# First-level blocks formed from pair weights, loop turned one level earlier, and reordered borders in a two-branch streaming layer

## The reference

```python
m   = beta[..., :, None] * einsum('bhnid,bhnjd->bhnij', k, k) * dec_strict
sol = triangular_solve(m + eye(C), rhs, left_side=True, lower=True, unit_diagonal=True)
```

## Time and profile before

| what | us |
|---|---|
| median of three runs | 2516.7 (2510.77 to 2518.69) |
| the profiled execution | 2527.18 |
| its span, first to last instruction | 2525.3 |
| PE busy | 2439.6 (97% of the span) |
| PEld (weight loads, beside PE) | 2281.4 |
| DVE busy | 1099.5 |
| POOL busy | 815.6 |
| ACT busy | 684.5 |
| mean granted clock of PE | 0.986 of full |

### The profile page before, as it was taken

The page is one execution under the profiler, slowest core; times in us unless marked ns, Lnnn a source line. Parts: engine busy times, 40 slices in busy tenths (PEclk is TensorE's granted clock), DMA queues, the critical chain, the costliest instruction groups (busy, mean ns, idle before and its releaser), DMA issues. The chain is left out here.

```text
span 2525.3 us, 38180 instructions
## 1 busy us (share of the span) xinstructions
PE 2439.6 (97%) x14883; PEld 2281.4 (90%) x14883; DVE 1099.5 (44%) x1849; ACT 684.5 (27%) x1378; POOL 815.6 (32%) x710
## 2 busy tenths in 40 slices
PE   7999999999999999999999999899999979999998
PEld 7989999999999999998989889798989979999886
DVE  6620111223476662015656556465656544325333
ACT  6211111110155521112332233232223242213222
POOL 1212211211111212214555455364545413334222
PEclk9989999999999999999999999899999989999999
DMA  5213512101111122423224324522432075553543
GB/s 165 74 69 111 214 51 76 43 34 60 43 52 67 61 77 95 121 71 85 82 83 117 112 80 125 177 79 83 125 104 82 32 267 193 192 178 122 161 140 106
DMA packets 200995, 265.82 MB, mean 105 GB/s; under 512 B 16272, under 2 KB 176288, under 8 KB 195360
## 3 DMA queue, kind: packets, MB, share of 16 engines
q1 hardware_dynamic: 200864, 263.86, 32.3%
HBM read 164.54 MB, written 99.29 MB: 104 GB/s over the span
## 5 line engine op out<-in xcount | busy, mean ns | idle before, releaser
L390 PE MATMUL dense<-h,w_hi 128*128 128x416 f32 (+1 forms) x1640 | 591.4, 361 | 0.0
L391 PE MATMUL dense<-h,w_hi 128*128 128x416 f32 (+1 forms) x1640 | 582.8, 355 | 0.0
L392 PE MATMUL dense<-h,w_lo 128*128 128x416 f32 (+1 forms) x1640 | 582.2, 355 | 0.0
L185 POOL TENSOR_TENSOR w_hi<-w_raw,zero 128x1024 fp32r<-128x1024 f32 x77 | 148.3, 1925 | 1134.9 <-PE dense L392 797.6
L1434 PE MATMUL gate_bank<-h,w_hi 128*128 128x352 f32 x1632 | 427.0, 344 | 26.1 <-issue 19.8
L390 PEld LDWEIGHTS dense<-h,w_hi 128*128 128x128 f32 x1640 | 310.6, 189 | 14.0 <-issue 5.6
L391 PEld LDWEIGHTS dense<-h,w_hi 128*128 128x128 f32 x1640 | 309.4, 189 | 11.3 <-issue 4.5
L392 PEld LDWEIGHTS dense<-h,w_lo 128*128 128x128 f32 x1640 | 309.6, 189 | 7.1
L1434 PEld LDWEIGHTS gate_bank<-h,w_hi 128*128 128x128 f32 x1632 | 276.5, 192 | 35.5 <-issue 26.4
L1434 PE MATMUL gate_bank<-h,w_lo 128*128 128x352 f32 x816 | 266.6, 327 | 0.0
L2408 PE MATMUL y<-o_hi,wo_hi 128*128 128x352 f32 x576 | 188.6, 328 | 16.6 <-DVE prod L2467 8.2
(11 more groups left out here) (237 smaller groups left out, 3940.9 us busy)
## 6 DMA issues: line engine op xcount, KB each, us to landing
w_raw<-in_w_in SPq DMA_DIRECT2D x77, 512.0 KB, 6.0
rows_then_inputs<-scratch_feat SPq DMA_DIRECT2D x16, 1856.0 KB, 9.1
scratch_feat<-row_y SPq DMA_DIRECT2D x28, 1056.0 KB, 4.8
gate<-scratch_gates SPq DMA_DIRECT2D x12, 2112.0 KB, 8.5
scratch_gates<-gate_row SPq DMA_DIRECT2D x102, 176.0 KB, 1.9
o_raw<-scratch_branch_out SPq DMA_DIRECT2D x6, 2112.0 KB, 13.3
scratch_h_second<-h SPq DMA_DIRECT2D x2, 4224.0 KB, 19.4
h<-scratch_h_second SPq DMA_DIRECT2D x6, 1408.0 KB, 7.9
```

Of the source, the lines that this page charges most:

```text
L185: nc.gpsimd.tensor_tensor(self.hi[:, p], raw, zeros, ALU.add).then_inc(self.high_ready, 1)
L390: nc.tensor.matmul(out, w_hi[:, p, k], hi.tile(k, t), start=(k == 0), stop=False)
L391: nc.tensor.matmul(out, w_hi[:, p, k], lo.tile(k, t), start=False, stop=False)
L392: mm = nc.tensor.matmul(out, w_lo[:, p, k], hi.tile(k, t), start=False, stop=(k == KD - 1))
```

## The change

It has five parts.

1. **Level 0 without a transpose.** POOL forms `pair_w` for the next chunk: decay under a mask that keeps a token's own pair in both directions (with a minus sign), times the beta of the pair's second token. DVE multiplies KK in PSUM by `pair_w` (`pair_m`, two instructions, ahead of `KK_taken`), and forms XT and X from `pair_m` by a per-token factor (even or odd token) plus the identity. PE's four transposes, the buffer X0 and the instructions at L1902, L1906 and L1910 are gone. PE's level 1 waits for `XT_ready`. For the beta of the pair's second token, the special rows get four more rows: ACT's exponential and DVE's add and reciprocal run over rows 64 to 99 in place of 64 to 67, and one copy on DVE is added.
2. **The loop's turn** stands before level 3 (`TURN_LEVEL` 3) in place of before level 4.
3. **The start**: the first token tile's products may stand behind the fifth turn in place of the sixth.
4. **The exchange of h**: `good(0)` comes ahead of the wait for the gates and the load of part 2; `good(2)` comes directly behind the stores of the outputs, ahead of the loads for the next chunk.
5. **The border to the closing phase**: the low part of the second branch's o moves from the chunk phase's end to the closing phase's start; tile 0's gates are loaded in three pieces behind wo(2) in place of ahead of it, and opened in pieces (`open_first`); the linear attention's states are stored by two transfers in place of four.

Its core:

```diff
-        while todo and len(now) < STEPS and j >= -(-span(todo[0][0]).stop // P) - 1 + 2:
+        while todo and len(now) < STEPS and j >= -(-span(todo[0][0]).stop // P) - 1 + (2 if todo[0][0] else 1):
...
                     for T in range(TILES):
                         r, t = T // 3, T % 3
+                        if swap and T == TILES - 1:
+                            good(0)
                         if swap and r == 1:
                             sp.wait_ge(gate_ready, c * TILES + (T + 1))
                             load_h(t)
-                        if swap and T == TILES - 1:
-                            good(0)
...
-                def outputs(c, tok, p):
+                def outputs(c, tok, p, between=None):
                     store(c, tok)
+                    if between is not None:
+                        good(between)
                     load(tok + 2, p)
...
-                TURN_LEVEL, OPENING_STEPS = 4, 26
+                TURN_LEVEL, OPENING_STEPS = 3, 23
...
                             if l == 1:
-                                now(pe, "m0t_taken", c)
+                                now(pe, "XT_ready", c)
...
                         gate_products(4)
-                        now(pe, "M0_ready", c)
-                        now(pe, "vt_taken", c)
-                        for h in range(HEADS):
-                            mm = transpose(ring[1][0:n, h, 0:n], X0[0:n, h, 0:n], ident[0:n, 0:n])
-                        mm.then_inc(S["m0t"], 1)
                         now(pe, "kt_taken", c)
...
+                def pair_weights(c, i, p, n):
+                    now(pool, "dec_ready", c)
+                    now(pool, "gb_taken", c)
+                    before(pool, "KK_taken", c)
+                    for a, done in ((0, "pair_upper"), (HALF, "pair_lower")):
...
+                            tt(pair_w[q], dec[q, :, q], mask.to_broadcast([HALF, HEADS, HALF]), ALU.mult) \
+                                .then_inc(S[done], 1)
...
+                    tt(pair_w[0:n], pair_w[0:n], beta.to_broadcast([n, HEADS, HALF]), ALU.mult) \
+                        .then_inc(S["pair_w_ready"], 1)
...
                     if then is not None:
+                        pair_weights(*then)
                         queries(*then)
...
+                    now(dve, "pair_w_ready", c)
+                    for q in quarters:
+                        last = tt(pair_m[q], ring[2][q, :, q], pair_w[q], ALU.mult)
                     last.then_inc(S["KK_taken"], 1)
...
                     for q in quarters:
-                        last = tt(X0[q, :, q], M[q, :, own_quarter], quarter_over_heads(masks[q, M_LOW + q.start:M_LOW + q.stop]),
-                                  ALU.mult)
-                    last.then_inc(S["M0_ready"], 1)
-                    now(dve, "m0t", c)
-                    tt(XT[0:n, :, 0:n], over_heads(ident[0:n, 0:n]), ring[1][0:n, :, 0:n],
-                       ALU.subtract).then_inc(S["m0t_taken"], 1)
-                    now(dve, "M0_ready", c)
-                    for q in quarters:
-                        last = tt(X[q], quarter_over_heads(ident[q, q]), X0[q, :, q], ALU.subtract)
+                        stt(XT[q, :, q], pair_m[q], masks[q, M_TOKEN + 1:M_TOKEN + 2],
+                            quarter_over_heads(ident[q, q]), ALU.mult, ALU.add)
+
+                    last = nc.vector.memset(XT[0:HALF, :, HALF:P], 0.0)
+                    last.then_inc(S["XT_ready"], 1)
...
+                    last = stt(X[0:n], pair_m[0:n], masks[0:n, M_TOKEN:M_TOKEN + 1],
+                               same.to_broadcast([n, HEADS, HALF]), ALU.mult, ALU.add)
...
-        dve.wait_ge(self.o_high, 2)
-        difference(self.o_lo[1], late.o_raw[:, 4:8], self.o_hi[1]).then_inc(self.o_split, 1)
...
                     if first:
                         next_wo(2)
+                        late.load_gate_rows(sp, d, slice(0, 6), late.first_gates_landed)
                         next_wo(3)
+                        late.load_gate_rows(sp, d, slice(6, 12), late.gate_landed[0])
+                        late.load_gates(sp, d, 0, 1)
...
-                for half in range(2):
-                    late.load_gates(sp, d, 0, half)
                 tile(0, first=True)
...
                 o_part(0, 2)
                 weights_high(1)
-                open_gates(0, 0)
                 weights_high(2)
+                open_first(slice(0, 6), late.first_gates_landed)
                 weights_high(3)
+                open_first(slice(6, 12), late.gate_landed[0])
                 open_gates(0, 1)
...
                 nc.vector.memset(eps[:, :], EPS).then_inc(eps_set, 1)
+                low(0, 1)
                 low(0, 2)
                 weights_low(1)
```

More of the change, by code:

```diff
@@ L1157, in chunk_phase @@
         own_quarter = slice(HALF, P)
-        X0 = sb("X0", [P, HEADS, P])
+        pair_w = sb("pair_w", [P, HEADS, HALF])
+        pair_m = sb("pair_m", [P, HEADS, HALF])
         X = sb("X", [P, HEADS, HALF])
@@ L1328, in store_states @@
                     sp.dma_start(d[gdn].rearrange("h d v -> d h v"), state[:, :, :]).then_inc(state_stored, 16)
-                    for h in range(HEADS):
-                        sp.dma_start(d[gla][h], gla_state[half_of(h), h]).then_inc(state_stored, 16)
+                    for q in range(2):
+                        sp.dma_start(d[gla][q::2].rearrange("h d v -> d h v"), gla_state[half_of(q), q::2]) \
+                            .then_inc(state_stored, 16)
                 for t in range(3):
@@ L1362, in _ @@
                 gate_traffic(CHUNKS // 2, 0, 1, swap=True)
[L1363 to L1366, removed]
+                good(1)
+                outputs(CHUNKS // 2, CHUNKS // 2 - 1, 0, between=2)
                 with sp.Fori(CHUNKS // 4, CHUNKS // 2 - 1) as i:
@@ L1572, in closing @@
                         now(pe, "QF_ready", c)
+                        now(pe, "vt_taken", c)
                         before(pe, "dSg_taken", c)
@@ L1811, in _ @@
                 pool.wait_ge(masks_landed, 16)
+                pair_weights(*SAMPLE)
                 queries(*SAMPLE)
@@ L2071, in load_gates, with load_gate_rows @@
             .then_inc(self.gate_landed[half], 16)
+    def load_gate_rows(self, sp, d, rows, landed):
+        sp.dma_start(self.gate[:, 0, rows], d["gates"][:, rows, 0:BT]).then_inc(landed, 16)
     def load_in_chunk_phase(self, sp, d):
@@ L2357, in statistics, with open_first @@
                                          scale=-0.5).then_inc(rstd_ready, 1)
+                def open_first(rows, landed):
+                    act.wait_ge(landed, 16)
+                    nc.scalar.activation(gate[:, 0, rows], gate[:, 0, rows], ACT.Sigmoid).then_inc(first_open, 1)
                 o_part(0, 2)
                 weights_high(1)
-                open_gates(0, 0)
                 weights_high(2)
+                open_first(slice(0, 6), late.first_gates_landed)
                 weights_high(3)
+                open_first(slice(6, 12), late.gate_landed[0])
                 open_gates(0, 1)
@@ L2460, in gated @@
                     dve.wait_ge(y_ready, t * KD + (m + 1))
-                    if m % 4 == 0:
-                        dve.wait_ge(gates_open, t * 2 + (m // 4 + 1))
+                    if first and m < 4:
+                        dve.wait_ge(first_open, m // 2 + 1)
+                    elif m % 4 == 0:
+                        dve.wait_ge(gates_open, t * 2 + m // 4)
                     if not (first and m < 2):
@@ L2635, in shape_constants @@
         if n == 0:
-            m[:, M_LOW:M_LOW + P] = low
+            own = (low | low.T).astype(np.float32)
+            m[:, M_PAIR:M_PAIR + HALF] = -np.concatenate([own[q, q] for q in (slice(0, HALF), slice(HALF, P))])
+            m[:, M_SAME:M_SAME + HALF] = np.tile(np.eye(HALF), (2, 1))
+            m[:, M_TOKEN], m[:, M_TOKEN + 1] = i % 2 == 1, i % 2 == 0
         m[:, M_PAIRS + n * HALF:M_PAIRS + (n + 1) * HALF] = low.T[:, i // s % 2 == 1]
@@ L2654, in laid_out @@
     special[:, AT_G:AT_G + 4] = w[:, 4112:4116]
-    special[:, AT_B:AT_B + 4] = w[:, 4116:4120]
+    for at in (AT_B, AT_PAIR):
+        special[:, at:at + 4] = w[:, 4116:4120]
     blocks[F_SPECIAL] = special.reshape(KD, P, P).transpose(1, 0, 2).reshape(P, DM)
```

46 lines of the change are left out of this document (29 added, 17 removed).

## The result

The changed kernel took 2484.01 us (median of 4 runs, 2481.72 to 2484.93). The kernel before took 2510.77, 2516.7 and 2518.69 us in the runs beside it; a fourth took 4798.56 us, counts as slow and is left out. The ratio is 0.9879, 95% interval 0.9854 to 0.9905: 1.2% or some 30 us faster, where 17.2 us were forecast. The time lies under the stated range. The profiled execution of the changed kernel took 2481.72 us, its span is 2480.0.

A forecast was written before the change was run, and what follows sets the result against it. PE, busy for 97% of the span, was taken as the bound, so time is its instructions plus its waits. −7.3 − 1.4 − 3.5 − 5.0 = −17.2 us from 2516.7 gave 2499.5 us, range 2488 to 2510.

The forecast's parts named there:

- The loop's turn (0; −5 to +12): Six branches back of the loop, 19.8 us of waits: moving the branch one level changes nothing, 0 us, −5 to +12.
- the difference is carried over: Profiled execution lies 10.5 us over the median; the forecast takes its saving straight off the median, 2516.7 us.
- Rival 1: Waits at the exchange of h and closing-phase border vanish whole, none re-forms: about −27, so 2490 us; chance 0.15.
- Rival 3: `pair_m` on DVE is dear beside POOL: QK waits 1.3 us in 16 chunks, +20.8, so 2520 us; chance 0.04.
- Transposes, −7.3: PE's four transposes per chunk, 0.44 us each time, go; their replacement stays hidden and QK does not wait: −7.3 us.
- The start, −1.4: First products behind the fifth turn; the ninth turn then limits, second tile's products at 37.9 for 39.32: −1.4 us, 0 to −3.3.
- The exchange, −3.5: Exchange of h: PE's waits for SP mostly go, but a wait for the next inputs forms: −3.5 us, 0 to −8.
- The border, −5.0: Border to closing phase: 1.5 us less there, block 2's wait goes, 4.3 us forms at block 4: −5.0 us, −2 to −10.

The follow-up runs named there:

- the further step: Changed kernel with tile 1's o loaded behind wo(5) and, in the exchange of h, the wide input load ahead of the wait for part 2: 2479.23 us.

## Why the prediction was wrong

The step that failed is **"The loop's turn (0; −5 to +12)"**: "the branch moves one level; its instructions and the number of branches stay", so no term. The six branch waits were in the first row that I read the earlier trace rows, 19.8 us, and I took them as the price of a branch. They were the price of a fetch, and the fetch depended on where the loop lay. In the traces this one term is 27 us where six passes were fetched, as in the execution that I worked from, and 10 us where two were, as in the second. In the medians it is some 16 to 18 us of the 29 to 30, what the other parts leave: 5.4 for the transposes, 3.7 for the exchange, 3.4 for the border and nothing for the start, 12.5 in place of the 17.2 forecast (an estimate, since it draws on three sets of runs). So the terms that I priced came out too high in sum, and the one at zero made up for more than that. Even −5 was too narrow a lower end, since the row itself bounds it at −19.8 with nothing known of its cause.

The same cause bears on what I passed over with "the difference is carried over", the 10.5 us by which the profiled execution lay above the median: of the 19.8 us between the spans of the two traces of that kernel, 17.1 lie in the six passes. How many passes an execution at the median fetches is not shown.

Rival 1, the borders' waits gone whole, came nearest in time, 2490, but not by its mechanism: both waits re-formed, as forecast. Rival 3 is out: the two `pair_m` took 0.86 us, about twice the 0.41 of the earlier trace rows and just over the 0.68 to 0.82 that I allowed. POOL was at work beside them, but with `sq_gla`; its split of the weights, which rival 3 names, had ended at 1322.78. Each of the 33 `pair_m` of the run took 0.42 to 0.43 us. DVE in one chunk of the changed kernel:

```profile
1321.59 2.64 DVE L1921 SCALAR_TENSOR_TENSOR M<-ring,decay_beta,dec 64x64 f32<-64x64 f32 x8 [3.28 <-PE ring L1533]
1324.24 0.86 DVE L1926 TENSOR_TENSOR pair_m<-ring,pair_w 64x256 f32<-64x256 f32 x2
...
1325.73 1.54 DVE L1933 SCALAR_TENSOR_TENSOR XT<-pair_m,masks,constants 64x256 f32<-64x256 f32 x2
```

and QK there:

```profile
1325.15 1.16 PE L1549 MATMUL ring<-rows_then_inputs 128*128 128x128 f32 x8
```

**Transposes, −7.3 forecast, −5.4 measured.** The row's 0.44 us is right, but the slack of 0.91 us ahead of QK was used up: `pair_m` ends at 1325.10, QK starts at 1325.15 and takes 1.16 us where it took 1.05. I had said that QK does not wait; it waits 0.1 us in a chunk, inside its first product, and the chunk's 0.34 is the 0.44 less that. POOL's part was mis-sized as well, hidden all the same:

```profile
1306.27 3.47 POOL L1785 TENSOR_TENSOR pair_w<-dec,masks 64x256 f32<-64x256 f32 x2
1309.82 0.61 POOL L1793 TENSOR_TENSOR pair_w<-pair_w,decay_beta 128x256 f32<-128x256 f32 x1
...
1318.44 1.89 POOL L188 TENSOR_TENSOR w_hi<-w_raw,zero 128x1024 fp32r<-128x1024 f32 x1 [0.57 <-PE gate_bank L1443]
```

4.1 us where I had 2.2; the idle time behind `queries` shrank from 2.63 us to 0.57. The two products of 64x256 took 1.7 us each; I took the price of `q_state`.

**The start, −1.4.** The trace follows the working, with the ninth turn at 37.14 where I had 37.1 and the seventh at 31.67 for 32.1:

```profile
27.39 1.04 PE L421 MATMUL turned<-constants,row_y 128*128 128x128 f32 x8
...
31.67 1.04 PE L421 MATMUL turned<-constants,row_y 128*128 128x128 f32 x8
...
37.14 1.09 PE L421 MATMUL turned<-constants,row_y 128*128 128x128 f32 x8 [1.29 <-DVE row_y L765]
```

In the runs without this part the time did not change, so the 1.3 us are not visible in the end. The rest of the 3.2 us by which the chunk phase began earlier in the trace lies at a stretch of half clock near 135 us, 3.4 us long after and 6.8 before; both lengths occur among the kernels with the new start and among those with the old one.

**The exchange, −3.5.** It came out at −3.7 in the runs. PE's wait for SP went, and the wait for the next inputs formed behind it, by DVE's first read (before at 1616.38):

```profile
1594.37 0.74 DVE L1853 TENSOR_TENSOR_SCAN F<-constants,rows_then_inputs 128x128 f32<-128x128 f32 x2 [3.56 <-DMA rows_then_inputs<-scratch_feat]
```

```profile
1595.71 0.67 PE L1523 MATMUL level_bank<-Z,X 128*64 128x64 f32 x8 [2.53 <-DVE Z L1977]
```

2.53 us, where I had put 2.7.

**The border, −5.0.** The runs give −3.4. The wait at block 2 went; the one at block 4 formed behind wo(4), as worked out, but 5.40 us long where I had 4.3. ACT's cast of wo(4), then DVE, then PE:

```profile
2022.33 1.47 ACT L2340 CAST wo_hi<-wo_ring 128x1536 fp32r<-128x1536 f32 x1 [4.41 <-DMA wo_ring<-in_wo]
```

```profile
2023.83 1.76 DVE L2490 TENSOR_TENSOR wo_lo<-wo_ring,wo_hi 128x1536 fp32r<-128x1536 f32 x1 [12.51 <-ACT wo_hi L2340]
2025.51 1.25 DVE L2508 TENSOR_TENSOR prod<-y,gate 128x1056 f32<-128x1056 f32 x1
```

```profile
2026.90 0.63 PE L2447 MATMUL y<-o_hi,wo_hi 128*128 128x352 f32 x1 [5.40 <-DVE prod L2508]
```

wo(4) was in 26.8 us after the first issue at 1995.55 (my sum gave 24.9). With tile 1's o loaded later, as in the further step, that wait was 2.11 us, so the o ahead of wo(4) did hold it up, as the sum had it. The border's own part was right: 8.12 to 6.58.

## What to carry to other kernels

A wait named "issue" behind a loop's branch need not be the price of the branch: look at the instruction queue's packets pass by pass, and count the instructions between two branches. Here a loop of some 1660 instructions was fetched anew in each pass, in some or in none, by where it lay; moving code ahead of it, or a few instructions out of it, decided more than what the instructions themselves cost. Where runs of one kernel spread far more than another's, ask what varies before taking one execution's waits as given.

## What the runs showed that I had not expected

The fetch is not the same in each execution of one kernel: 109 packets in one, 73 in another, and the kernel's runs lay between 2497.55 and 2527.73 us, while the changed kernel stayed within 3.2 us in either set. And padding a kernel with instructions that do nothing removed its fetches: 128 of them took away 54 packets, and a pass of 107.43 us took 102.97.
